# Two-layer pooling and Mamba-2 trunk, 512 tokens: the output written with tokens on partitions

## The reference, cut to what matters

```python
def rms_norm(x, g):
    y = x * rsqrt(mean(x * x, axis=-1, keepdims=True) + 1e-5)
    return y * g

h = h + sq_relu_mlp(rms_norm(h, norm_mlp_g[1]), mlp_w1[1], mlp_w2[1])   # 1024 -> 4096 -> 1024
return rms_norm(h, final_g)                                             # output (1, 512, 1024)
```

## Time and profile before

| | |
|---|---|
| median of 3 runs | 1116.74 us (1116.57 to 1117.53) |
| profiled execution, its own time | 1117.23 us |
| span of the profiled execution | 1115.4 us |
| mean granted clock of PE | 0.996 of full |
| PE busy | 1099.7 us, 99% of the span |
| DVE, ACT, POOL busy | 562.7, 460.9, 574.5 us |
| last matmul of the MLP (L719) ends, in the span | 1101.1 us |
| stores of the output | 8 of 256 KB |

### The profile page before, as it was taken

The page is one execution under the profiler, slowest core; times in us unless marked ns, Lnnn a source line. Parts: engine busy times, 40 slices in busy tenths (PEclk is TensorE's granted clock), DMA queues, the critical chain, the costliest instruction groups (busy, mean ns, idle before and its releaser), DMA issues.

```text
span 1115.4 us, 15303 instructions
## 1 busy us (share of the span) xinstructions
PE 1099.7 (99%) x5138; PEld 899.6 (81%) x5138; DVE 562.7 (50%) x664; ACT 460.9 (41%) x791; POOL 574.5 (52%) x438
## 2 busy tenths in 40 slices
PE   8999999999999999999999999999999999999996
PEld 6788888888888788788787887888888888888885
DVE  6755421455423384674856846466654124554213
ACT  7433222233333338557486664343332222333331
POOL 3666544445565645436354364546665444545551
PEclk9999999999999999999999999999999999999998
DMA  7223232222223225332433333222222222222222
GB/s 265 95 96 101 90 104 98 94 94 94 95 94 100 98 81 141 123 131 97 137 100 123 132 101 102 92 95 94 94 94 95 95 102 100 98 94 95 94 94 75
DMA packets 39428, 117.03 MB, mean 105 GB/s; under 512 B 4064, under 2 KB 10848, under 8 KB 39392
## 3 DMA queue, kind: packets, MB, share of 16 engines
q1 hardware_dynamic: 38960, 115.70, 31.1%
q10 hardware_dynamic: 432, 0.86, 0.2%
HBM read 114.32 MB, written 2.23 MB: 104 GB/s over the span
## 4 chain that ended last, share of the span: by engine, by line
PE 96%; DVE 2%; ACT 1%; DMA 0%; issue 0%; POOL 0%; DVEq 0%; ACTq 0%
PE bank L717 30%; PE bank L719 30%; PE bank L718 30%; PE bank L908 1%; PE bank L917 1%; PE bank L925 1%; PE bank L867 1%; PE bank L767 1%; DMA x_token<-x_tok 0%; DVE x_lo L987 0%; ACT x_hi L434 0%; DVE scaled_residual L1345 0%; PE bank L885 0%; PE bank L751 0%; ACT residual L440 0%
## 5 line engine op out<-in xcount | busy, mean ns | idle before, releaser
L617 POOL TENSOR_TENSOR w_lo<-w_raw,w_hi 128x512 fp32r<-128x512 f32 x372 | 495.4, 1337 | 486.8 <-ACT w_hi L387 486.8
L387 ACT ACTIVATE w_hi<-w_raw 128x512 fp32r<-128x512 f32 x372 | 231.0, 627 | 431.1 <-PE bank L719 429.6
L717 PE MATMUL bank<-x_hi,w_hi 128*128 128x512 f32 x848 | 336.4, 397 | 2.8 <-DVE x_lo L987 1.9
L719 PE MATMUL bank<-x_hi,w_lo 128*128 128x512 f32 x848 | 330.3, 390 | 0.0
L718 PE MATMUL bank<-x_lo,w_hi 128*128 128x512 f32 x848 | 330.2, 389 | 0.0
L717 PE MATMUL bank<-act_hi,w_hi 128*128 128x512 f32 x640 | 252.1, 394 | 0.0
L719 PE MATMUL bank<-act_hi,w_lo 128*128 128x512 f32 x640 | 249.1, 389 | 0.0
L718 PE MATMUL bank<-act_lo,w_hi 128*128 128x512 f32 x640 | 249.0, 389 | 0.0
L717 PEld LDWEIGHTS bank<-x_hi,w_hi 128*128 128x128 f32 x848 | 159.2, 188 | 40.7 <-issue 6.6
L718 PEld LDWEIGHTS bank<-x_lo,w_hi 128*128 128x128 f32 x848 | 159.3, 188 | 34.8 <-issue 2.6
L719 PEld LDWEIGHTS bank<-x_hi,w_lo 128*128 128x128 f32 x848 | 159.2, 188 | 33.4
(11 more groups left out here) (133 smaller groups left out, 656.3 us busy)
## 6 DMA issues: line engine op xcount, KB each, us to landing
w_raw<-weights SPq DMA_DIRECT2D x186, 512.0 KB, 3.3
m<-acs_scratch SPq DMA_DIRECT2D x16, 512.0 KB, 4.2
decay_in<-eacs_scratch SPq DMA_DIRECT2D x24, 128.0 KB, 3.7
x_token<-x_tok SPq DMA_DIRECT2D x4, 512.0 KB, 7.2
residual<-xt SPq DMA_DIRECT2D x8, 256.0 KB, 10.5
out_t<-scaled_residual SPq DMA_DIRECT2D x8, 256.0 KB, 2.4
pooling_matrices<-pooling ACTq DMA_DIRECT2D x1, 576.0 KB, 5.3
constants<-consts SPq DMA_DIRECT2D x1, 208.0 KB, 10.3
```

What stands on the lines that cost most here:

```text
L387: act.activation(whi[:, c % 2, part], raw[:, c % 2, part], ACT.Copy).then_inc(hi_ready, 1)
L617: pool.tensor_tensor(wlo[:, c % 2, part], raw[:, c % 2, part], whi_f[:, c % 2, part], ALU.subtract).then_inc(lo_ready, 1)
L717: pe.matmul(out, wh, xh, start=start, stop=False)
L719: return pe.matmul(out, wl, xh, start=False, stop=stop)
```

## The change

The output is written with tokens on partitions. PE transposes the tiles of hg into banks: for each chunk c of 128 tokens and each half of the channels (four tiles of 128) one bank, eight banks' worth in seven banks, as `TOKEN_BANK` says. DVE or ACT multiplies each bank by the factor of its partition, r_tok, while it copies it to the new buffer `output_rows`, which lies where x_hi was. SP stores each half row block into an output of `[4, 128, 1024]`: 128 pieces of 2 KB, 4 KB apart in DRAM.

The order on PE is now: sums over square_sum into four columns of bank 7 (`statistic_by_token`), transposes of tiles 0 to 3 for all four chunks, sums over the last square into the same columns, transposes of tiles 4 to 7. The first sums are drained by DVE into `mean_rest` before the second ones overwrite them; DVE then adds the two. The diagonals and their products with ones are gone. DVE scales six of the banks, ACT two. In full, without the declarations of semaphores:

```diff
+TOKEN_BANK = {(0, 0): 2, (1, 0): 3, (2, 0): 4, (3, 0): 5, (0, 1): 6, (1, 1): 1, (2, 1): 0, (3, 1): 2}
+BY_VECTOR = [(0, 0), (1, 0), (2, 0), (3, 0), (2, 1), (3, 1)]
+BY_SCALAR = [(0, 1), (1, 1)]
+ROWS_ORDER = [(0, 0), (1, 0), (2, 0), (3, 0), (0, 1), (1, 1), (2, 1), (3, 1)]
+STORES = [(0, 0), (0, 1), (1, 0), (1, 1), (2, 0), (3, 0), (2, 1), (3, 1)]
+
...
-        xhi, _ = sb("x_hi", [P, KD, TOK], F32R)
+        xhi, o_xhi = sb("x_hi", [P, KD, TOK], F32R)
+        rows, _ = sb("output_rows", [P, CHUNKS, D_MODEL], F32, o_xhi)
+        mean_rest, _ = sb("mean_square_of_first_tiles", [P, CHUNKS])
...
-            for m in range(KD):
-                sp.wait_ge(out_ready, m + 1)
-                sp.dma_start(out_t[m, :, :], hg[:, m, :]).then_inc(out_written, 16)
-            sp.wait_ge(out_written, 16 * KD)
+            for c, half in STORES:
+                if (c, half) in BY_SCALAR:
+                    sp.wait_ge(rows_scalar, BY_SCALAR.index((c, half)) + 1)
+                else:
+                    sp.wait_ge(rows_vector, BY_VECTOR.index((c, half)) + 1)
+                part = slice(TOK * half, TOK * half + TOK)
+                sp.dma_start(out_t[c, :, part], rows[:, c, part]).then_inc(out_written, 16)
+            sp.wait_ge(out_written, 16 * len(STORES))
...
+            act.wait_ge(inverted, 5)
+            for c, half in BY_SCALAR:
+                act.wait_ge(rows_ready, ROWS_ORDER.index((c, half)) + 1)
+                act.activation(rows[:, c, TOK * half:TOK * half + TOK], bank[TOKEN_BANK[c, half]][:, :], ACT.Copy,
+                               scale=r_tok[:, c:c + 1]).then_inc(rows_scalar, 1)
...
+            statistic_by_token()
+
+            def to_rows(c, m):
+
+                return pe.transpose(bank[TOKEN_BANK[c, m // 4]][:, P * (m % 4):P * (m % 4) + P],
+                                    hg[:, m, P * c:P * c + P], ident)
+
+            pe.wait_ge(hg_ready, 4)
-                pe.matmul(bank[2 + c][:, 0:1], ssq[:, P * c:P * c + P], ones[:, 0:1], start=True, stop=False)
+                for m in range(4):
+                    last = to_rows(c, m)
+                last.then_inc(rows_ready, 1)
+            pe.wait_ge(rest_mean, 1)
-                last = pe.matmul(bank[2 + c][:, 0:1], sq[:, 1, P * c:P * c + P], ones[:, 0:1],
-                                 start=False, stop=True)
+                last = pe.matmul(b_stat[:, c:c + 1], sq[:, 1, P * c:P * c + P], ones[:, 0:1], start=True, stop=True)
+            pe.wait_ge(hg_ready, KD)
+            pe.wait_ge(acc_drained, A_MLP1 + 48)
-                pe.wait_ge(diag_ready, CHUNKS * GROUPS + c + 1)
-                last = pe.matmul(b_stat[:, P * c:P * c + P], ones, diag[:, P * c:P * c + P], start=True, stop=True)
-            last.then_inc(spread_ready, 1)
+                if c == CHUNKS - 1:
+                    pe.wait_ge(rows_vector, 1)
+                for m in range(4, KD):
+                    last = to_rows(c, m)
+                last.then_inc(rows_ready, 1)
...
-            for c in range(CHUNKS):
-                last = dve.tensor_scalar(r_tok[:, c:c + 1], bank[2 + c][:, 0:1], 1.0 / D_MODEL, EPS,
-                                         ALU.mult, ALU.add)
-            last.then_inc(stat_drained, 1)
-            make_diagonals(6)
-            dve.wait_ge(spread_ready, GROUPS + 1)
-            for m in range(KD):
-                dve.wait_ge(hg_ready, m + 1)
-                dve.tensor_tensor(hg[:, m, :], hg[:, m, :], b_stat[:, :], ALU.mult).then_inc(out_ready, 1)
+            dve.tensor_scalar(mean_rest[:, :], b_stat[:, 0:CHUNKS], 1.0 / D_MODEL, EPS, ALU.mult, ALU.add
+                              ).then_inc(rest_mean, 1)
+            dve.wait_ge(rest_mean, 1)
+            dve.wait_ge(stat_ready, 9)
+            dve.scalar_tensor_tensor(out=r_tok[:, :], in0=b_stat[:, 0:CHUNKS], scalar=1.0 / D_MODEL,
+                                     in1=mean_rest[:, :], op0=ALU.mult, op1=ALU.add).then_inc(stat_drained, 1)
+            dve.wait_ge(sqrt_done, 6)
+            dve.reciprocal(r_tok[:, :], r_tok[:, :]).then_inc(inverted, 1)
+            dve.wait_ge(inverted, 5)
+            for c, half in BY_VECTOR:
+                dve.wait_ge(rows_ready, ROWS_ORDER.index((c, half)) + 1)
+                dve.tensor_scalar(rows[:, c, TOK * half:TOK * half + TOK], bank[TOKEN_BANK[c, half]][:, :],
+                                  r_tok[:, c:c + 1], None, ALU.mult).then_inc(rows_vector, 1)
...
-    out_t = nc.dram_tensor("out_t", [KD, P, TOK], F32, kind="ExternalOutput").ap()
+    out_t = nc.dram_tensor("out_t", [CHUNKS, P, D_MODEL], F32, kind="ExternalOutput").ap()
-    return np.ascontiguousarray(r.results[0]["out_t"].reshape(D_MODEL, TOK).T)[None]
+    return np.ascontiguousarray(r.results[0]["out_t"].reshape(TOK, D_MODEL))[None]
```

More of the change, by code:

```diff
@@ L258, in build @@
         hg_ready = sem("scaled_ready")
-        out_ready = sem("out_ready")
+        rest_mean = sem("mean_of_first_tiles")
+        rows_ready = sem("output_rows_transposed")
+        rows_vector = sem("output_rows_scaled_vector")
+        rows_scalar = sem("output_rows_scaled_scalar")
         out_written = sem("out_written")
```

## The result

The changed kernel took 1129.64 us (median of 4 runs, 1129.53 to 1130.33), the kernel before 1116.76 us beside it. The ratio is 1.0115, with an interval of 1.0103 to 1.0127. The forecast was 1114.6 us, in a range of 1113.7 to 1116.0.

What follows compares the result with a forecast made beforehand. The chain is 96% PE, the end bound by store transfers. First issue 2.12 us earlier (2.03 + 0.19 - 0.1) takes the profiled 1117.23 to 1115.1; the median, 0.49 lower, gives 1114.6 us, range 1113.7 to 1116.0.

Steps and rivals of the forecast that it cites:

- The step that failed: Matmul body before the tail: untouched by the change, so only what follows the second MLP's last matmul can move.
- A body of another length: Sign of a wrong prediction: the body before 1101 us has another length than before; no chance given.
- Sixteen transposes ahead of the sums, 0.1 us: PE queue before the last token sums: 1.7 of 1.74 us fall into an idle gap; cost 0.1 us, bounds 0.05 and 0.3.
- Mean by one operation: DVE after the token sums: four operations, 0.36 us together, become one of 0.17 us; gain 0.19 us.
- Diagonals and spread gone, 2.03 us: Between reciprocal and first product: 2.07 us of diagonals and spread matmuls become a wait of 0.04 us.
- Output from the banks: DVE and ACT scale banks from 1105.33 us, about 0.69 us each on DVE, with no ACT table load; later transposes delay nothing.
- Stores: Kernel's end: first issue at 1106.05 us, then 5.5 us of transfers at 380 GB/s as before; transfers stay the limit.
- Both rate rivals: Output transfers: slower stores, 1118.1 us at 233 GB/s, 5%; faster stores, 1114.2 us at 416 GB/s, 17%.
- The sum of the tail: First store issue moves from 1108.17 to 1106.05 us: 2.12 us, from 2.03 diagonals and spread, 0.19 mean, -0.1 queued transposes.
- the fall at 1106: Trace of the kernel before: granted clock 1.00 until 1106 us, 0.63 on average in the next microsecond.
- The clock rival: Tail on PE: clock falls to 1.2 GHz before 1102 us, slowing transposes and sums; 1116.9 us, no change; 3%.

Runs made afterwards that it cites:

- repaired change: Changed kernel with unused bytes behind mean_rest, so act_hi and all behind move by 256 bytes instead of 32: 1114.42 us, ratio 0.9975.
- both repaired versions: Changed kernel with mean_rest allocated last, or left in place with act_hi and all behind moved by 256 bytes: 1114.42 us each, ratio 0.9975.
- the sums first: Changed kernel at the 256-byte distance, with all 32 transposes behind the token sums of the last square instead of 16 ahead: 1116.78 us.

## Why the prediction was wrong

*The step that failed* is the first one: "The matmul body is untouched by this change, so only what follows the last matmul of the second MLP can move." The code is untouched, the addresses are not. The prediction put the body at nothing, and it lost 14.97 us: 5.9 ns on each of the 2544 products with x, because act and the weights had moved by 32 bytes against x. The cost of a 16-byte buffer was never asked for: it stood in the diff, ahead of act_hi and the weights, and the prediction spent all its rivals on the tail. A body of another length stood only among the signs of an error, without a chance or a price. That the distance is the cause is shown by the runs with unused bytes; why the distance matters is not.

*Sixteen transposes ahead of the sums, 0.1 us:* right. They are 0.111 us apart, sums 0.10 later than before.

*Mean by one operation:* right, 0.16 us for 0.17.

*Diagonals and spread gone, 2.03 us:* right; from the reciprocal's end to the first output are 0.04 us instead of 2.07.

*Output from the banks:* right. No table load; ACT's two take 1.27 us, DVE's six 4.04. The last four transposes wait 0.2 us for bank 2 and delay nothing.

*Stores:* right in what counts, 5.5 us at 380 GB/s from the first data on, though the rows start 4 KB apart. An issue costs SP more, 0.51 us in the median (0.35 to 0.64) instead of 0.33, and this is hidden, since the last issue still ends at 1125.6, over a microsecond ahead of the last data. Both rate rivals fell. The Trainium skill, "DMA: Bandwidth & Descriptors", section "Latency and other measured facts", lists 207 GB/s for copies between tensors in HBM at a row pitch of 512 KiB, 164 at 2 MiB and 103 at 4 MiB, against 214 with the last one padded. So its loss at 512 KiB is small, and a pitch of 4 KiB isn't in it; here the stores at 4 KiB show no loss.

*The sum of the tail:* 2.12 us forecast, 1.97 to 2.02 measured. The repaired change takes 1114.42 us, the forecast was 1114.6; its span is 1113.1 in the profiled run, forecast 1113.3. That the time comes within 0.2 us of the forecast is in part luck: the gain is larger than the 2.1 us forecast, and the kernel before took 1117.2 beside it, not 1116.7. That the medians differ by 2.8 us and not by 2.0 has the clock in it: in both repaired versions its mean is 0.998 to 0.999 in all runs, in the kernel before 0.994 to 0.996, with spans of 1115.5 to 1116.4 us at 0.994 and 1114.3 to 1115.1 at 0.996. The prediction noted the fall at 1106 and priced only an earlier one; that the change would end it was missing. Its size apart from the rest is not measured.

*The clock rival:* fell. It stayed at 1.00 until PE was done.

## What to carry to other kernels

A buffer inserted among others is a change to all that lie behind it; here one of 16 bytes cost PE's products 15 us, 1.4% of the kernel. Where the stream and the weights of the products come from different buffers, round every insertion up to 256 bytes, which cost nothing here, or put it last, and read the mean of the untouched products first when a small edit moves the time by a per cent. A prediction should go through the allocations of a diff as through its instructions.

## What the runs showed of the hardware

The fp32r products here (fp32r is the rounded type of the hi and lo buffers), 128 x 128 by 512 columns, start every 226.7 ns when the buffers of x_hi, x_lo, w_hi and w_lo lie whole multiples of 256 bytes apart (tiles inside them are 512 and 2048 bytes apart), and every 232 to 233.3 ns when w_lo or x_lo alone is 32 bytes off, or x 32, 64 or 128 bytes off the weights. That is up to 2.9% more for each product, 12.5 to 15.5 us where only the products of x are slow and 22 to 28 where those of act are too. The absolute address does not matter (1116.95 us with all buffers moved), nor do the smaller buffers behind the weights (1117.16 us with these moved). The Trainium skill, "TensorE: Matmul & The Clock Gate", section "Part 2: What happens when you issue a matmul", says that two independent read ports feed the stream and the weight load, so that loading the next weights takes no read bandwidth from the running product. These runs don't show whether the two ports get in each other's way, but what a product takes here does depend on how the addresses of the buffers that PE reads stand to each other. Why, and why the 20 ns of a group shift among its three products, is not shown; other distances than the ones above, bf16 and other sizes were not tried.

In the 256-byte version PE does nothing but transposes from 1101.5 to 1103.3, and the granted clock stays at 1.00; with the sums first it is idle there, and the clock is at 0.50 from 1104 to 1105. The same skill page, section "Part 4: PE-mode transpose", says of PE's transposes that they don't count as PE being busy in the same way, and that the full clock doesn't engage for them. The pair of runs speaks against that here. The clock's fall in a gap is not certain either: in four of the ten runs with the sums first the mean clock is 0.999 to 1.000 and the span 1113.2 to 1113.4, with the same code.
